# Gate units moved out of the attention rounds into paired block products, with values two slots behind the turn

## What is computed

```python
u = jnp.einsum('bsd,dn->bsn', rms_norm(x, g_pre), w_in)      # 1024 x 1024 by 1024 x 8192
(pool_v, pool_g, conv_x, conv_gb, conv_gc, conv_g,
 sb_q, sb_k, sb_v, sb_g, merge) = jnp.split(u, _split_points(), axis=-1)   # ten of 512 columns, merge of 3072
y_pool = pool_mixer(pool_v, pool_w, pool_scale) * jax.nn.silu(pool_g)
y_conv = conv_mixer(conv_x, conv_gb, conv_gc, conv_w, conv_b) * jax.nn.silu(conv_g)   # gate_b * (conv(gate_c * x) + b)
y_sb = stick_breaking_attention(sb_q, sb_k, sb_v) * jax.nn.silu(sb_g)      # 8 heads of 64, 1024 tokens
proj = jnp.einsum('bsnw,nwd->bsnd', jnp.stack([y_pool, y_conv, y_sb], axis=2), w_branch)
merged = jnp.sum(jax.nn.sigmoid(merge.reshape(b, s, N_BRANCH, D_MODEL)) * proj, axis=2)
```

## Time and profile before

| | |
|---|---|
| runs before | 2385.47, 2387.70, 2388.01 us; median 2387.7 |
| profiled execution | 2387.61 us, span of its instructions 2385.8 us |
| TensorE (products) | busy 2290.8 us, 96% of the span |
| VectorE | busy 1545.0 us, 65% |
| ScalarE | busy 946.5 us, 40% |
| GpSimd | busy 317.7 us, 13% |
| granted TensorE clock, mean | 0.990 of full speed |

### The profile page before, as it was taken

The page is one execution under the profiler, slowest core; times in us unless marked ns, Lnnn a source line. Parts: engine busy times, 40 slices in busy tenths (PEclk is TensorE's granted clock), DMA queues, the critical chain, the costliest instruction groups (busy, mean ns, idle before and its releaser), DMA issues. The chain is left out here.

```text
span 2385.8 us, 31843 instructions
## 1 busy us (share of the span) xinstructions
PE 2290.8 (96%) x11560; PEld 1909.0 (80%) x11560; DVE 1545.0 (65%) x2014; ACT 946.5 (40%) x1589; POOL 317.7 (13%) x305
## 2 busy tenths in 40 slices
PE   7999999999999999999999799988999999999997
PEld 6888888887788877887878688876887888888885
DVE  4555555565855446558788787764688777775557
ACT  4434343443333322343444445543433333334443
POOL 0111111121000000002232455440011000000000
PEclk9999999999999999999999999999999999999999
DMA  3111111110333363423332421203325343438664
GB/s 140 45 55 36 45 64 45 55 45 29 122 106 105 125 245 135 147 108 120 105 107 90 140 80 53 66 13 108 113 99 201 151 154 149 171 133 303 222 184 170
DMA packets 102618, 273.36 MB, mean 115 GB/s; under 512 B 9356, under 2 KB 35180, under 8 KB 98028
## 3 DMA queue, kind: packets, MB, share of 16 engines
q1 hardware_dynamic: 102508, 271.88, 32.9%
HBM read 196.03 MB, written 75.81 MB: 114 GB/s over the span
## 5 line engine op out<-in xcount | busy, mean ns | idle before, releaser
L94 PE MATMUL psG<-h_hi,w_hi 128*128 128x512 f32 (+1 forms) x880 | 224.6, 394 | 2.0 <-DVE features_T L1815 1.6
L94 PE MATMUL psG<-h_hi,w_lo 128*128 128x512 f32 (+1 forms) x880 | 223.2, 391 | 0.0
L94 PE MATMUL psG<-h_lo,w_hi 128*128 128x512 f32 (+1 forms) x880 | 222.9, 392 | 0.0
L94 PEld LDWEIGHTS psG<-h_hi,w_hi 128*128 128x128 f32 x880 | 159.4, 189 | 35.6 <-issue 3.0
L94 PEld LDWEIGHTS psG<-h_lo,w_hi 128*128 128x128 f32 x880 | 160.3, 189 | 30.6
L94 PEld LDWEIGHTS psG<-h_hi,w_lo 128*128 128x128 f32 x880 | 159.2, 188 | 30.0
L409 POOL TENSOR_TENSOR sb_w<-sb_left 128x128 f32<-128x128 f32 (+3 forms) x96 | 89.1, 931 | 469.7 <-DVE sb_left L552 463.7
L560 DVE TENSOR_TENSOR sb_w_lo<-psT,sb_w_hi 128x512 fp32r<-128x512 f32 (+1 forms) x80 | 50.7, 634 | 146.9 <-ACT sb_w_hi L434 146.8
L124 DVE TENSOR_TENSOR w_lo<-w_raw,w_hi 128x1024 fp32r<-128x1024 f32 x62 | 75.6, 1222 | 95.5 <-ACT w_hi L119 95.3
L426 ACT ACTIVATE sb_left<-psA 128x128 f32<-128x128 f32 (+3 forms) x96 | 47.1, 491 | 184.7 <-PE psA L694 113.5
L119 ACT CAST w_hi<-w_raw 128x1024 fp32r<-128x1024 f32 x64 | 67.2, 1051 | 125.1 <-PE psG L94 75.9
(11 more groups left out here) (608 smaller groups left out, 5721.9 us busy)
## 6 DMA issues: line engine op xcount, KB each, us to landing
w_raw<-in_units SPq DMA_DIRECT2D x100, 512.0 KB, 3.8
w_raw<-hidden_blocks SPq DMA_DIRECT2D x77, 256.0 KB, 2.9
merge_gates<-features_T SPq DMA_DIRECT2D x12, 1024.0 KB, 7.5
merge_gates<-merge_gates SPq DMA_DIRECT2D x12, 1024.0 KB, 4.8
features<-features_T SPq DMA_DIRECT2D x24, 512.0 KB, 3.9
w_spare<-in_units SPq DMA_DIRECT2D x22, 512.0 KB, 4.2
hidden_blocks<-features_T SPq DMA_DIRECT2D x11, 1024.0 KB, 3.9
down_sums<-w_spare SPq DMA_DIRECT2D x22, 512.0 KB, 3.3
```

Of the source, the lines that this page charges most:

```text
L94: return pe.matmul(out, lhs, rhs, start=first, stop=last, skip_group_check=True)
```

## The change

- The 16 gate units (pool_g, conv_gb, conv_g and sb_g of each channel block) are no longer made in the rounds. They become 8 further halves ahead of the 10 (`GATED` = 8), in pairs pool_g with sb_g and conv_gb with conv_g. The ungated mixer results go to DRAM in the rounds, come back during these halves (`load_before_gate`, into the idle weight buffers), VectorE multiplies (`times_gates`, two multiplications of 1024 columns a half) and SP stores the result (`store_gated`).
- The remaining 24 units are listed in `ROUND_UNITS`: 6, 6, 5 and 4 units in the four rounds, that is 6, 6, 5 and 4 groups a slot (12, 12, 10, 8 products). The tables `DONE_AT`, `CONV_AT`, `SCALE_AT`, `POOL_AT`, `TURN_IN`, `MIX_IN` say in which slot what happens. Pool windows that would be multiplied by zero are left out (1, 2, 3, 4 windows instead of four each); two sets of windows are in round 3.
- `values` stand two slots behind the turn. `wT`, `w_hi` and `w_lo` are double; for that the logits have one bank `A`.
- `MOVE_AT` becomes 12, 20, 24, 32, so the group's first values still stand in the slot behind. `gate_add` writes the result; `gate_times` is gone.
- All channel parameters and pool weights are loaded once, at the start of SP's list.
- The explicit loads of the sigmoid table on ACT are gone.

The core of the diff:

```diff
-MOVE_AT = [[m + LATER[i] for m in (11, 19, 23, 31)] for i in range(NC4)]
+MOVE_AT = (12, 20, 24, 32)
+ROUND_UNITS = (("conv_x", "gate_c", "pool_v", "q", "k", "v"), ("conv_x", "gate_c", "pool_v", "q", "k", "v"),
+               ("conv_x", "gate_c", "q", "k", "v"), ("pool_v", "pool_v", "conv_x", "gate_c"))
+PER_SLOT = [len(r) for r in ROUND_UNITS]
...
+DONE_AT = {}
+for _u in range(3, len(UNITS)):
+    DONE_AT.setdefault(slot_of(24 * _u + 23), []).append(_u)
+POOL_AT = ((12, 13), (NS + 12, NS + 13, NS + 14), (3 * NS + 6, 3 * NS + 7, 3 * NS + 8, 3 * NS + 9),
+           (3 * NS + 14, 3 * NS + 15, 3 * NS + 16, 3 * NS + 17, 3 * NS + 18))
...
-        A = [ctx.enter_context(nc.psum_tensor(f"psA{s}", [P, HALF], F32)) for s in range(2)]
-        wT = ctx.enter_context(nc.psum_tensor("psT", [P, HALF], F32))
+        A = ctx.enter_context(nc.psum_tensor("psA", [P, HALF], F32))
+        wT = [ctx.enter_context(nc.psum_tensor(f"psT{s}", [P, HALF], F32)) for s in range(2)]
...
+            sp.dma_start(par, chan.rearrange("c p n -> p c n")).then_inc(par_here, 16)
+            sp.dma_start(pw, pool_w.rearrange("c p n -> p c n")).then_inc(par_here, 16)
+            for c in range(2, 7):
                 W.load(sp, c)
```

VectorE's list in the rounds after the change, and what changes in TensorE's and in the halves:

```diff
             for S in range(N_CHUNKS + TAIL - 1):
                 i, s = divmod(S, NS)
                 if 1 <= S < N_CHUNKS + 1:
                     scan(S - 1)
                 for n in BACKS_AT[S]:
                     low_weights(n)
                 for r, g in due(MOVE_AT, S):
                     gate_add(dve, r, g)
+                if i < NC4 and s in TURN_AT:
+                    turn_v(i, TURN_AT.index(s))
+                for k in range(NC4):
+                    for n, at in enumerate(POOL_AT[k]):
+                        if S == at:
+                            pool_window(k, n) if n <= k else pool_mean(k)
+                    if 0 <= S - CONV_AT[k] < 3:
+                        conv_taps(k, S - CONV_AT[k])
+                    if S == SCALE_AT[k]:
+                        scale_pool(k)
+                for u in DONE_AT.get(S, ()):
+                    W.split_lo(dve, u + 2)
...
                 logits(S)
-                if S:
-                    for n in BACKS_AT[S - 1]:
+                if S >= 2:
+                    for n in BACKS_AT[S - 2]:
                         values(n)
...
-MERGE_HALVES, MERGE_PLAIN = 10, 28
+GATE_PAIRS = ((1, 9), (3, 5))
+GATED = 2 * NC4
+MERGE_HALVES, MERGE_PLAIN = GATED + 10, 28
...
+            def times_gates(m):
+                gate_done(dve, 12, m, 0)
+                dve.wait_ge(before_here[m % 2], 32 * (m // 2 + 1) if m < NC4 else 16 * (NC4 + m // 2 - 1))
+                rows, y = hid[m % 2], before_gate(m)
+                if m < NC4:
+                    for r in range(2):
+                        TT(rows[:, r, :], rows[:, r, :], y[r], ALU.mult).then_inc(y_gated, 1)
+                else:
+                    TT(rows[:, 0, :], rows[:, 0, :], rows[:, 1, :], ALU.mult).then_inc(y_gated, 1)
+                    dve.wait_ge(y_gated, 2 * m + 1)
+                    TT(rows[:, 0, :], rows[:, 0, :], y[0], ALU.mult).then_inc(y_gated, 1)
```

More of the change, by code:

```diff
@@ L309, in layer1_mixers @@
         of_head = lambda ap, h: ap.rearrange("p (k h) d -> p h k d", h=2)[:, h]
[L311 to L322, removed]
         def due(table, S):
-            return [(r, g) for r in range(NC4) for g in range(4) if NS * r + table[r][g] == S]
+            return [(r, g) for r in range(NC4) for g in range(4) if NS * r + table[g] == S]
         def row_chunk(S):
@@ L366, in store_attention @@
         def store_attention(sp, i):
-            sp.wait_ge(o_gated, 4 * i + 4)
+            sp.wait_ge(o_read, 4 * i + 4)
             sp.dma_start(y_out[2 * NC4 + i], y[2]).then_inc(y_stored[2], 16)
         def gate_add(dve, i, g):
-            h = g // 2
-            part = o_sum[own(h), :]
+            qt, h = g % 2, g // 2
             dve.wait_ge(o_moved, 4 * i + g + 1)
[L375 to L383, removed]
+            if g == 0 and i:
+                dve.wait_ge(y_stored[2], 16 * i)
@@ L385, in _ @@
+            dve.tensor_tensor(y[2][own(h), qt * HALF:(qt + 1) * HALF], O[own(h), :], o_sum[own(h), :], ALU.add).then_inc(o_read, 1)
         @block.sync
         def _(sp):
-            for c in range(2, 5):
+            sp.dma_start(par, chan.rearrange("c p n -> p c n")).then_inc(par_here, 16)
+            sp.dma_start(pw, pool_w.rearrange("c p n -> p c n")).then_inc(par_here, 16)
+            for c in range(2, 7):
                 W.load(sp, c)
[L389 to L399, removed]
+            for S in range(N_CHUNKS + TAIL):
+                for u in DONE_AT.get(S, ()):
+                    if u + 4 < UNIT0["merge"] + 2:
+                        W.load(sp, u + 4)
+                for k in range(NC4):
+                    if S == SCALE_AT[k] + 1:
+                        entry_out(sp, ENTRY["mix", k])
+                        sp.dma_start(y_out[k], y[0]).then_inc(y_stored[0], 16)
+                    if S == CONV_AT[k] + 3:
+                        sp.wait_ge(conv_done, k + 1)
+                        sp.dma_start(y_out[NC4 + k], y[1]).then_inc(y_stored[1], 16)
+                    if k < NC4 - 1 and S == NS * k + MOVE_AT[3] + 1:
+                        store_attention(sp, k)
@@ L431, in high_weights @@
                 act.wait_ge(w_turned, n + 1)
[L432 to L447, removed]
+                if n >= 2:
+                    act.wait_ge(pv_done, n - 1)
+                act.copy(w_hi[n % 2][:, 0:m], wT[n % 2][:, 0:m]).then_inc(w_hi_done, 1)
             def stack_q(h):
@@ L469, in move_out, with evacuate @@
                 if 4 * i + g:
-                    act.wait_ge(o_gated, 4 * i + g)
+                    act.wait_ge(o_read, 4 * i + g)
                 act.copy(o_sum[own(h), :], O[other(h), :]).then_inc(o_moved, 1)
[L473 to L476, removed]
-                    return
[L478 to L487, removed]
-                    act.copy(pv[0][:, PAD:], g[:]).then_inc(out, 1)
[L489 to L494, removed]
+            def evacuate(u):
+                kind, k = UNITS[u]
+                e = ENTRY[kind, k]
+                g, out = buffer_of(e), emptied(e)
+                if kind == "gate_c":
+                    return
+                entry_full(act, e)
+                if kind == "q":
+                    if k:
+                        act.wait_ge(stack_lo, 6 * k)
+                    act.mul(q_next, g[:], SB_SCALE).then_inc(out, 1)
+                elif kind == "k":
+                    if k:
+                        act.wait_ge(stack_lo, 6 * k)
+                    act.copy(k_next, g[:]).then_inc(out, 1)
+                elif kind == "v":
+                    if k:
+                        entry_out(act, ENTRY["turn", k - 1])
+                    act.copy(v_next, g[:]).then_inc(out, 1)
+                elif kind == "pool_v":
+                    if k:
+                        act.wait_ge(pooled, 2 * k)
+                    act.copy(pv[0][:, PAD:], g[:]).then_inc(out, 1)
+                elif kind == "conv_x":
+                    if k:
+                        act.wait_ge(y_stored[1], 16 * k)
+                    act.copy(cx, g[:]).then_inc(out, 1)
@@ L496, in _ @@
             act.copy(ident_r[:], C["ident"][:]).then_inc(consts_r, 1)
             act.activation(not_before[:], C["upto"][:], ACT.Copy, scale=NEG).then_inc(consts_r, 1)
[L498 to L502, removed]
+            for u in range(3):
+                entry_full(act, u)
+                W.split_hi(act, u + 2)
+                evacuate(u)
+                if u == 1:
                     entry_out(act, 0)
@@ L632, in _ @@
                 dve.memset(left[s][:, left[s].shape[1] - 1:], 1.0).then_inc(pads, 1)
-            for c in range(2, U0 + 2):
-                W.split_lo(dve, c)
-                if c == U0:
+            for u in range(3):
+                W.split_lo(dve, u + 2)
+                if u == 1:
                     stack_low_q(0, 0)
@@ L888, in in_order @@
             start()
-            half(0, 0)
-            half(1, 0)
-            with eng.Fori(0, (H - 4) // 2) as i:
-                half(2, i)
-                half(3, i)
+            for m in range(GATED + 2):
+                half(m, 0)
+            with eng.Fori(0, (H - GATED - 4) // 2) as i:
+                half(GATED + 2, i)
+                half(GATED + 3, i)
             half(H - 2, 0)
@@ L950, in end @@
                 sp.wait_ge(a_lo_done, 7 * (H - 1) + 7)
-                for b in range(3):
-                    sp.wait_ge(L1.y_stored[b], 16 * NC4)
+                for m in range(GATED - 2, GATED):
+                    free_pair(sp, m + 2, 0)
                 for c in range(NC4):
@@ L3488, in layouts @@
     w1 = column_units(np, I["w_in"][0])
-    order = [24, 28, 32]
-    for c in range(NC4):
-        order += [4 * s + c for s in (0, 1, 2, 9, 4, 3, 5)]
-        if c < NC4 - 1:
-            order += [4 * s + c + 1 for s in (6, 7, 8)]
```

(6 more changed lines are left out.)

343 lines of the change are left out of this document (177 added, 166 removed).

## The result

| | before | after |
|---|---|---|
| median, us | 2386.91 (4 runs) | 2397.44 (4 runs, 2395.53 to 2399.14) |
| ratio | 1 | 1.0045, 95% interval 1.0034 to 1.0057 |
| profiled execution, span | 2387.61, 2385.8 | 2395.53, 2393.8 |
| TensorE busy | 2290.8 us | 2276.6 us |
| VectorE busy | 1545.0 us | 1596.5 us |

The kernel became slower, by 10.5 us or 0.45%. TensorE is busy 14.2 us less and ends 8.0 us later in the profiled execution, so it stands still for some 22 us more than before. Time at its lower clock counts as busy here and comes on top: it is part of why TensorE's busy time fell by less than the 22.3 us of products that went.

The account below looks back on a forecast made before the run. The prediction took TensorE's work to bound the kernel. Its terms, -22.3 + 27.0 + 0.8 + 0.2 + 1.5 + 0 + 11.3 = +18.5 on the profiled 2387.6, gave 2406 us, range 2373 to 2417.

Parts of the forecast that it names:

- Removed and given back: TensorE's products: 16 gate units leave the rounds (174.6 us), 8 halves of 19.04 us come back; net -22.3 us.
- Waits on O in the rounds: In the shortened slots TensorE waits for gate_add to free the single accumulator bank; 27.0 us over four rounds.
- the chain at a border: Where a unit ends at slot start, evacuation, split_lo, scan, low part and gate_add free O only after 5.9 us.
- The clock: TensorE's clock falls behind longer waits on O: four at 1.5 us, half of seven more; 11.3 us, between 0 and 16.5.
- the sum of 2411: Total in us if, by the Trainium skill, all eleven waits of 1.8 us or longer paid a clock fall.
- Logits: With one logits bank, slot 1's logits wait for the first sigmoid behind its table load; 0.8 us.
- the turn in round 3: In round 3 the turn of the values follows an evacuation closely; 0.2 us.
- The third unit's weights: At the start, parameter and pool-weight loads ahead on SP's queue make these weights late; 1.5 us, 0 to 4.
- Tail and start of the merge: Behind the rounds, waits of 0.28 and 3.04 us go, one of about 3.6 comes, one turn less; 0.
- The first one, that the handover is in time: Rival: gate_add isn't behind split_lo, so no clock is lost; 2375 us, 2366 without waits; chance 0.25.
- The second, that the waits come and the clock holds: Rival: TensorE waits on O in the rounds without a clock fall; 2395 us, or 2388 with shorter waits; chance 0.18.
- The last round didn't tip over: Rival for round 3: VectorE, at 67 of 74 us, gets longer scans and windows; 2417 us and above; chance 0.07.

Follow-up runs that it names:

- e5: Changed kernel with two more waited-for VectorE passes of 1024 columns in each of the 8 new halves: 2397.90 us.
- e1: Changed kernel with gate_add moved first in VectorE's slot, ahead of the scan and the low part: 2365.98 us.
- e2: Changed kernel with split_hi and split_lo moved to the end of the slot where a unit ends just ahead of a handover of O: 2374.32 us.
- e4: Changed kernel with gate_add done twice, with a wait between, at each handover of O: 2419.13 us.
- e3: Changed kernel with gate_add first in its slot and the splits at the slot's end where a unit ends on a handover's border: 2359.19 us.

## Why the prediction came out as it did

Forecast 2406 with a range of 2373 to 2417, measured 2397.4. The direction and the mechanism were right, and the forecast was 8.6 us high. Profile against profile it is +18.5 forecast and +7.9 measured; by its own terms:

- *Removed and given back, -22.3.* Right. Eight halves cost 152.3 us again, TensorE doesn't wait in them, and e5 shows that they are covered.
- *Waits on O in the rounds, +27.0.* Measured 23.9, at the 14 places named. The forecast of the chain at a border was 5.9 us and it is 5.8; TensorE's arrival was put at 3.8 and is 4.0. By round, forecast against measured: 3.9 and 3.4; 7.9 and 7.2; 5.0 and 4.7; 10.2 and 8.6. In round 2 two misses cancel: slot 12 was put at 0.55 and took 1.07, slot 20 at 1.5 and took 1.05. The largest miss is round 3, where two waits put at 3.0 took 2.3 and 2.15; ahead of them 0.35 and 0.34 had already been spent in a wait of the logits, which is part of it. That `gate_add`'s place behind `split_lo` and scan is the cause is shown by e1 and e2, each of which takes away one half of the queue ahead of it.
- *The clock, +11.3.* This is the term that was mis-sized most: 6.8 us in the rounds. It was four falls of 1.7 us each, where the forecast had the worth of seven and a half of 1.5; so the number of falls was too high, and the price of one a little low, since it was read from a single stretch of 3 us. Counting waits of 2.3 us and more fully and those of 1.8 to 2.1 by half did not hold either: two of the four and two of the seven paid. The granted clock fell behind four waits of the rounds, 1.82, 1.99, 2.29 and 2.30 us, and stayed at its upper level (2.4 GHz) behind 1.83, 1.86, 2.15 and 2.31. Two rows of the changed kernel, columns as in the earlier trace rows, behind waits of 1.99 and 1.83:

```profile
162.00:165.00 3.00, 3.00 (x11) 2.38 (x11) 0.56 (x1) 1.21 (x2) 0.13 (x1) 0.60 0.00 0
...
109.00:112.00 3.00, 3.00 (x17) 2.46 (x16) 1.93 (x5) 0.48 (x1) 0.40 (x1) 1.00 0.00 0
```

The Trainium skill (TensorE: Matmul & The Clock Gate, HAM oscillation) has a loop that idles the array once per pass pay the fall in every pass; its loop waits some 3 to 5 us for a transfer each time, longer than any wait of the rounds here, which the prediction passed over. Here four of the eight waits of 1.8 us or more paid, so "every" doesn't carry over to such shorter waits; the sum of 2411 that it gave was further off than 2406. In e4, where the waits are 0.7 longer, the loss doubled.

- *Logits, +0.8.* 1.7 us: 0.56 at 62.64, as foreseen, and three more of 0.34 to 0.48 at other logits. The one bank costs more than the first place of it; the 0.2 for the turn in round 3 was not seen.
- *The third unit's weights, +1.5.* No wait: the start took 58.84 us instead of 58.98. The issues of parameters and pool weights ahead of them did not make them late.
- *Tail and start of the merge, 0.* The tail has the wait of 3.8 (forecast 3.6) and is 1.1 us shorter. The four plain units take 33.1 us instead of 641.54 - 606.21 = 35.3, since the wait ahead of the block products went from 2.5 to 0.3; VectorE's last `split_lo` there ends 2.1 us sooner. The first halves after them no longer run at a lower clock: with the tail's, that loss went from 3.4 to 1.7 us. With the eighteen halves 0.8 us under the forecast, that is 4.2 us up to their end that I had not counted.

In the rounds the terms are -174.6 + 23.9 + 1.7 + 6.8 = -142.2, or -143.1 with the 0.9 us of waits that the last round had before and has no more, where the stage shows -139.3; 3.8 us of it are not assigned. From the tail to the end of the halves it is +148.1 instead of +152.3, and what follows them is 0.7 us shorter. The rest up to the +10.5 us of the medians is the spread of executions: the profiled one was the fastest of its four, at a mean clock of 0.989 where the others have 0.986 and 0.987. More waits may have brought a fall in those; they have no trace that would show it.

The rivals: the first one, that the handover is in time, describes e1 to e3, not this kernel; its price for it (2375, or 2366 with no waits) was too high, since e3 reaches 2359; the time saved behind the rounds, which the prediction didn't count, can account for most of that. The second, that the waits come and the clock holds (2395), is nearer to the measured number than my forecast, but not what happened: the clock did fall. The last round didn't tip over; its waits are the largest of a round, 8.6 us, and e1 and e3 remove most of them, so they came from the order and not from too much work on VectorE.

## What to carry to other kernels

When products leave a pipelined loop, its slots shorten, and every chain that ended inside one has to be added up again, from the start of the slot to the releaser and along the in-order queue of each engine on the way; most of the price is what stands ahead of the releasing instruction (here all but 0.7 of 5.8 us), not the instruction. Here the change paid for itself only after the one instruction that frees the single accumulator was put first in its slot (two moved lines: 2397 to 2366 us), ahead of the scan and of the low part, which itself waits for ScalarE. Where a transfer of work saves 1%, look for one or two microseconds of wait per pass in the loop that it leaves, and count the clock beside it.

## What the runs showed of the hardware

- **The clock behind short waits.** Waits of nearly the same length fell on both sides (1.82 fell and 1.83 did not, 2.30 fell and 2.31 did not; in e4, 2.29 fell, and 3.04, ended at 403.40, did not). So the length of a wait alone does not decide. Where the loss was summed it went, for waits on O of 27.7, 11.4, 4.3 and 1.4 us (changed kernel, e2, e1, e3), as 8.6, 3.4, 1.7 and 0 us; at 38.5 us (e4) it was 18.8. It came in steps: each fall cost 1.7 us, but for two in e4, behind waits of 3.02 and 4.54 us, that cost 3.4 each.
- **GpSimd beside VectorE.** The 128x512 difference on POOL took 1.20 us on average in the changed kernel and 1.46 in e3. Most took about 1.0; 9 of the 48 were over 1.8 us in the changed kernel and 17 in e3, the longest 5.04 in both. The one of 3.73 at 106.70 in e3's rows above ran while VectorE went without a gap through a low part, a pool window of 1024 columns (107.12), `split_lo` and a scan. Rows of the groups by line and shape, POOL, 59 to 575 us, of the changed kernel:

```profile
L421 POOL TENSOR_TENSOR sb_w<-sb_left 128x512 f32<-128x512 f32 x48 | 57.3, 1198 | 197.1 <-DVE sb_left L548 197.1
```

and of e3:

```profile
L425 POOL TENSOR_TENSOR sb_w<-sb_left 128x512 f32<-128x512 f32 x48 | 69.9, 1460 | 171.6 <-DVE sb_left L553 171.6
```

It held up nothing that TensorE waits for. Spans on POOL are rough in this view, and no run here was made to find the cause.
